# Three changes in a one-core decoder step: an eleven-slot expert ring, an output projection in split products, and a new attention order

## The chip, the cores and the metric

The kernel runs on one core of a Trainium2 chip. The core has a matrix engine (PE in the profile), three engines for elementwise work (DVE, ACT, POOL), and a sequencer (SP) that here only issues DMA transfers. Each engine works through its own list of instructions in program order and meets the others at semaphores, counters that one instruction raises and another waits for. The metric is the device time of one execution in microseconds (us); less is better.

## The reference

One layer of a decoder for 512 prompt tokens and 32 sample tokens (8 sequences of 4, each with 256 cached positions), width 1024, all in float32:

```
h = x @ w_in                                  # 1024 -> 5632: retention q,k,v,g; attention q,k,v; gates a,b
o_r = groupnorm(retention(rq, rk, rv)) * silu(rg)          # 4 heads of 128
o_m = moba(mq, mk, mv)                                     # 8 heads of 64, softmax, past keys in pages
merged = sigmoid(a) * (o_r @ w_br_ret) + sigmoid(b) * (o_m @ w_br_moba)
x1 = layer_norm(ALPHA * x + merged @ w_out)                # the output projection
y  = layer_norm(ALPHA * x1 + moe(x1))                      # 32 experts, 1024 -> 128 -> 1024, 2 per token
```

## The kernel before

The 544 tokens stand as five row tiles (four of 128, one of 32). The stages follow each other.

**Projection of x** (0 to 197 us). Weights come in column tiles of 128. Each float32 operand is split into a high part in a rounded format (fp32r) and a low part, the rest; `split_weights` makes both on DVE. A product is then three matmuls, high by high, high by low and low by high (`split_products`, L677 to L679), each 272 token columns wide.

**Attention** (197 to 296 us). A list `ORDER`, written by hand, gives the steps, and PE, DVE and ACT each walk it and do their share, so its order is the order on all three. `S` is a score product (PE into one of four PSUM banks, DVE takes it out), `R` the normalization of exponentials on DVE, `T` the transposes of the probabilities on PE with a copy by ACT, `O` a product whose result DVE or ACT takes out, `W(m)` the split of weight tile m on DVE, `G(m)` its product on PE, `N` the normalization of the retention rows. The eight MoBA heads go as four pairs: `moba(p)` is the eight scores of pair p, `inv(p)` its `R` steps, `turned(p)` its eight transposes, `pv` its product with the values. `ret`, `rets` and `reto` are scores, state and output of a retention head; `samp`, `skv`, `cross`, `sampv` and `sel` belong to the samples.

**Gates and branches** (to 438 us). 24 tiles: gate a, gate b and branch (r) tiles in turn. PE needs some 6 us for each, DVE splits the next one meanwhile and, after a branch tile, `merge` writes one of the eight slices of `merged`.

**Output projection** (440 to 517 us). For each row tile, both halves of 512 columns and eight slices k, one plain float32 matmul at L928 with `merged` as the stationary operand and `w_out` as the moving one: 80 matmuls. DVE does the layer norm of tile t while PE is at tile t+1; `turn_x1` and `router` stand between on PE.

**Routing and experts** (517 to 678 us). Experts go in 16 pairs; pair n uses experts 2n and 2n+1, each 1.5 MB of weights, of which the gate and up part (1 MB, L634) and the down part (0.5 MB, L629) come by transfers of their own. Eight slots of a ring take experts 0 to 28 in turn; three more places (`cst`, `scratch` and `w_ring`, which are free by then) are loaded once, with experts 29, 30 and 31. Experts 0 to 2 and 31 are loaded while the projection runs, 3 to 7 once it is done, 29 and 30 once routing is known; a slot is refilled when PE is through with it. Token rows are gathered and results scattered by POOL. Then the rows are summed and normalized (to 717 us).

## Time and profile before

| what | value |
|---|---|
| median of three runs | 718.72 us (716.89 to 720.13) |
| time of the profiled execution | 718.71 us |
| span of that execution (first to last instruction) | 716.9 us |
| PE busy | 646.8 us (90%) |
| share of PE in the chain that ended last | 81% |

The span is what the trace shows; the execution's own time is 1.8 us longer, and what the change does to the span is added to that time. A busy PE is one with a matmul in flight; whether it is at its pace is read from the spacing of matmuls.

### The profile page before, as it was taken

To read this page: it belongs to the slowest core of one execution; us is meant where nothing else is said; L and a number is where in the kernel's file an instruction comes from. 1 tells how busy PE (TensorE), PEld (TensorE's weight loads), DVE (VectorE), ACT (ScalarE), POOL (GpSimd) and SP (SyncE) were. 2 spreads that over 40 slices of the span, in tenths; PEclk is the share of its full clock that TensorE was granted. 3 is DMA by queue.
4 is the path that set the end of the run, shared out by engine and by line. 5 is a ranking of instruction groups with operands and counts; after the bars stand their busy time and mean duration, and the time that the engine had idled before them with its cause. 6 is when DMAs were issued, how large, how long until landed. Compare 5 with 4: busy or idle time off the path is not lost.

```text
span 716.9 us, 10905 instructions
## 1 busy us (share of the span) xinstructions
PE 646.8 (90%) x4365; PEld 503.9 (70%) x4365; DVE 291.3 (41%) x585; ACT 133.6 (19%) x286; POOL 70.8 (10%) x74
## 2 busy tenths in 40 slices
PE   4999999999989988799999997999943899988996
PEld 3999999999955666699999995455343455454431
DVE  6344334353275577434444442333365112211235
ACT  0111101120083434300000010000110331312222
POOL 0101400030040000000000000000002133221213
PEclk9999999999999999899999999999955899999996
DMA  9425221227145362233444205900077999998163
GB/s 357 143 88 176 88 88 59 87 74 237 61 114 143 109 180 90 59 89 136 143 144 141 85 1 171 392 30 30 29 300 271 387 407 416 415 417 345 54 267 125
DMA packets 45479, 124.49 MB, mean 174 GB/s; under 512 B 6177, under 2 KB 19617, under 8 KB 41218
## 3 DMA queue, kind: packets, MB, share of 16 engines
q1 hardware_dynamic: 39392, 112.33, 43.4%
q0 software_dynamic: 4752, 8.93, 3.3%
q10 hardware_dynamic: 1298, 2.73, 1.0%
q8 instruction: 25, 0.41, 0.2%
q14 instruction: 12, 0.10, 0.0%
HBM read 114.72 MB, written 17.43 MB: 184 GB/s over the span
## 4 chain that ended last, share of the span: by engine, by line
PE 81%; DVE 8%; DMA 6%; ACT 2%; issue 2%; SPq 1%; POOLq 0%; DVEq 0%; ACTq 0%
PE ps L679 12%; PE ps L677 12%; PE ps L678 12%; PE ps L928 10%; PE ps L970 7%; PE ps L672 6%; PE ps L986 3%; DMA arena<-experts 3%; PE ps L1048 3%; PE ps L891 2%; PE ps L892 2%; PE ps L893 2%; PE ps L743 1%; PE ps L805 1%; PE ps L739 1%
## 5 line engine op out<-in xcount | busy, mean ns | idle before, releaser
L677 PE MATMUL ps<-xa_hi,w_hi 128*128 128x272 f32 x704 | 206.9, 294 | 10.4 <-DVE xa_lo L1370 10.4
L679 PE MATMUL ps<-xa_hi,w_lo 128*128 128x272 f32 x704 | 205.3, 292 | 0.0
L678 PE MATMUL ps<-xa_lo,w_hi 128*128 128x272 f32 x704 | 204.7, 291 | 0.0
L677 PEld LDWEIGHTS ps<-xa_hi,w_hi 128*128 128x128 f32 x704 | 134.7, 191 | 11.8 <-issue 9.8
L678 PEld LDWEIGHTS ps<-xa_lo,w_hi 128*128 128x128 f32 x704 | 134.9, 192 | 0.0
L679 PEld LDWEIGHTS ps<-xa_hi,w_lo 128*128 128x128 f32 x704 | 134.5, 191 | 0.0
L1361 DVE CAST w_hi<-w_ring 128x1024 fp32r<-128x1024 f32 x52 | 38.0, 730 | 121.1 <-PE ps L679 91.0
L928 PE MATMUL ps<-arena 128*128 128x512 f32 (+1 forms) x160 | 70.1, 594 | 2.3 <-issue 2.3
L970 PE MATMUL ps<-arena,work 128*64 128x256 f32 x464 | 60.3, 409 | 8.6 <-DMA arena<-experts 6.4
L1363 DVE TENSOR_TENSOR w_lo<-w_ring,w_hi 128x1024 fp32r<-128x1024 f32 x52 | 65.7, 1263 | 1.8
L970 PEld LDWEIGHTS ps<-arena,work 128*64 128x64 f32 x464 | 37.4, 147 | 27.2 <-issue 9.9
L928 PEld LDWEIGHTS ps<-arena 128*128 128x128 f32 (+1 forms) x160 | 27.3, 174 | 39.9 <-issue 39.8
L1303 POOL DMA_INDIRECT work<-x_rows,idx_i x13 | 13.3, 1027 | 374.4 <-DVE idx_i L1698 339.6
L891 PE MATMUL ps<-o_parts,w_hi 128*128 128x272 f32 x128 | 36.9, 289 | 1.6 <-DVE scratch L1543 1.6
L1381 DVE COPY arena<-ps 128x512 f32 x20 | 13.8, 690 | 59.7 <-PE ps L672 59.7
L893 PE MATMUL ps<-o_parts,w_lo 128*128 128x272 f32 x128 | 36.9, 288 | 0.0
L892 PE MATMUL ps<-o_parts,w_hi 128*128 128x272 f32 x128 | 36.9, 288 | 0.0
L1074 ACT ACTIVATE scratch<-ps 128x544 f32<-128x544 f32 x20 | 12.5, 624 | 126.6 <-PE ps L679 126.6
L1721 DVE COPY work<-ps 128x512 f32<-128x512 f32 x31 | 20.0, 686 | 36.5 <-PE ps L986 36.5
L1153 ACT ACTIVATE scratch<-ps,bm 128x544 f32<-128x544 f32 x16 | 11.5, 716 | 117.7 <-PE ps L679 117.7
L672 PE MATMUL ps<-cst,scratch 128*128 128x128 f32 (+1 forms) x180 | 27.9, 281 | 6.0 <-ACT arena L1121 3.7
L1715 DVE TENSOR_TENSOR work<-work,ps 128x128 f32<-128x128 f32 x16 | 4.6, 288 | 66.6 <-ACT work L1203 66.6
(222 smaller groups left out, 727.0 us busy)
## 6 DMA issues: line engine op xcount, KB each, us to landing
arena<-experts SPq DMA_DIRECT2D x29, 1024.0 KB, 15.9
w_ring<-w_tiles SPq DMA_DIRECT2D x52, 512.0 KB, 3.5
arena<-experts SPq DMA_DIRECT2D x29, 512.0 KB, 19.2
arena<-kT_pool SPq DMA_DIRECT2D x16, 256.0 KB, 3.1
out<-arena SPq DMA_DIRECT2D x4, 1024.0 KB, 5.9
arena<-v_pool SPq DMA_DIRECT2D x16, 256.0 KB, 2.9
arena<-w_out SPq DMA_DIRECT2D x4, 1024.0 KB, 5.6
arena<-token_rows SPq DMA_DIRECT2D x8, 512.0 KB, 6.5
```

The source lines that it names most:

```text
L672: return nc.tensor.transpose(out, in_, ident[0:rows, 0:rows])
L677: mm(out, w_hi[b][:, w], x_hi[:, k_x, cols], start=start, stop=False)
L678: mm(out, w_hi[b][:, w], x_lo[:, k_x, cols], start=False, stop=False)
L679: return mm(out, w_lo[b][:, w], x_hi[:, k_x, cols], start=False, stop=stop)
L891: mm(out, w_hi[m % 2][:, w], o_r[:, hi + k, cols], start=k == 0, stop=False)
L892: mm(out, w_hi[m % 2][:, w], o_r[:, lo + k, cols], start=False, stop=False)
L893: x = mm(out, w_lo[m % 2][:, w], o_r[:, hi + k, cols], start=False, stop=k == 3)
L928: m = mm(ps[0:r, 2 * (t % 2) + half, :], merged[:, k, t * P:t * P + r], wo[:, k, half * 512:(half + 1) * 512], start=k == 0, stop=k == KD - 1)
L970: m = mm(ps[s * CAP:(s + 1) * CAP, 2 + u, 0:2 * P], xgT[:, u, k, s * CAP:(s + 1) * CAP], wgu(slots[s], k), start=k == 0, stop=k == KD - 1)
L986: m = mm(ps[s * CAP:(s + 1) * CAP, 4 + 2 * u + half, :], hidT[:, u, s * CAP:(s + 1) * CAP], wd(slots[s], half), start=True, stop=True)
L1361: v.tensor_copy(w_hi[b][:], w_ring[:, j, :]).then_inc(s_hi, 1)
L1363: v.tensor_tensor(w_lo[b][:], w_ring[:, j, :], w_hi[b][:].bitcast(F32), ALU.subtract).then_inc(done, 1)
```

## The change

It does three things. (1) All eleven places for experts become one ring: expert e goes to place e modulo 11 (`SLOTS`), the place loaded early with expert 31 gets expert 10, the two loaded after routing get 8 and 9, and pair n's places are refilled with experts 2n+11 and 2n+12. PE's loop over pairs is written out. (2) The output projection takes split products: ACT writes the high parts of `w_out` (`wo_high`) and of `merged` (`merged_high`), DVE the low parts (`wo_low`, `merged_low`); five of the eight slices of `w_out` are split during the branch tiles, three after the last gate tile. (3) `ORDER` is new: retention heads come one pair earlier, `turned` is cut in two halves with other steps between, gate tile 0 and then tile 1 stand between the steps of the last pair (before, tile 0 alone stood near its end), with their weights in a buffer of their own (`w_buf`); the last pair's scores use two PSUM banks rather than four.

```diff
+SLOTS = 11
...
+        m_lo, = under(XT, [("merged_lo", [P, KD, T])])
+        wo_early, = under(WO, [("w_out_early", [P, 5, 2, D])])
...
+        wo_late, m_hi = under(0, [("w_out_late", [P, 3, 2, D]), ("merged_hi", [P, 2, KD, P])])
...
-        w_hi, w_lo = [w_hi0, w_hi1], [w_lo0, w_lo1]
+        w_hi, w_lo = [w_hi0, w_hi1, w_hi2], [w_lo0, w_lo1, w_lo2]
...
-        ORDER = ([("S", ("inner",))] + moba(0) + [("S", ("samp", 0))] + O("cross", 0) + inv(0) + skv(0)
-                 + [("R", ("samp", 0))] + turned(0)
-                 + moba(1) + ret(0) + O("pv", 0) + O("rets", 0) + inv(1) + [("T", ("samp", 0))] + O("reto", 0)
-                 + ret(1) + O("sampv", 0) + O("rets", 1) + turned(1) + O("sel", 0) + O("reto", 1)
-                 + moba(2) + ret(2) + O("pv", 1) + [("S", ("samp", 1))] + O("rets", 2) + inv(2) + O("cross", 1)
-                 + O("reto", 2) + ret(3) + [("R", ("samp", 1))] + turned(2) + O("rets", 3) + skv(1) + O("reto", 3)
-                 + moba(3) + O("pv", 2) + [("T", ("samp", 1)), ("N", ("std",)), ("W", (0,))] + inv(3) + O("sampv", 1)
-                 + [("N", ("rows",))] + turned(3) + O("sel", 1) + [("G", (0,))] + O("pv", 3))
...
+        ORDER = ([("S", ("inner",))] + moba(0) + [("S", ("samp", 0))] + O("cross", 0) + ret(0) + inv(0) + O("rets", 0)
+                 + turned(0, 0) + skv(0) + O("reto", 0) + turned(0, 1) + [("R", ("samp", 0))]
+                 + moba(1) + ret(1) + O("pv", 0) + [("T", ("samp", 0))] + O("rets", 1) + O("sampv", 0) + inv(1)
+                 + O("reto", 1) + turned(1, 0) + ret(2) + O("sel", 0) + turned(1, 1) + O("rets", 2) + O("reto", 2)
+                 + moba(2) + ret(3) + O("pv", 1) + [("S", ("samp", 1))] + O("rets", 3) + inv(2) + O("reto", 3)
+                 + turned(2, 0) + O("cross", 1) + skv(1) + turned(2, 1) + [("R", ("samp", 1))] + fill_weights(0)
+                 + moba(3) + O("pv", 2) + [("T", ("samp", 1)), ("N", ("std",))] + fill(0) + inv(3) + O("sampv", 1)
+                 + turned(3, 0) + fill_weights(1) + [("N", ("rows",))] + turned(3, 1) + fill(1) + O("sel", 1) + O("pv", 3))
...
+        LATE = S_IDX[("moba", 3, 0, 0)]
+
         def s_bank(jb):
-            return S_IDX[jb] % 4
+            return S_IDX[jb] % (4 if S_IDX[jb] < LATE else 2)
...
+        def w_buf(m):
+            return 2 if m == 0 or m % 2 == 1 else 1
+
+        def g_bank(m):
+            return 2 if m < 2 or TILES[m][0] == "b" else 0
...
+        def pair_slots(n):
+            return 2 * n % SLOTS, (2 * n + 1) % SLOTS
...
+                if 12 <= m <= 20 and m % 2 == 0:
+                    load_wo((m - 12) // 2)
+            sp.wait_ge(s_tile, M_OF[("b", KD - 1)] + 1)
+            for k in range(5, KD):
+                load_wo(k)
...
+            load_parts(10, experts_d[10])
...
+                load_parts(8 + s, experts_d[8 + s])
+            def next_experts(n):
+                return [e + SLOTS for e in (2 * n, 2 * n + 1) if e + SLOTS < NE]
...
+                for e in next_experts(n):
+                    sp.dma_start(expert(e % SLOTS)[:, 0:GU], experts_d[e][:, 0:GU]).then_inc(s_e[e % SLOTS], 16)
...
+                if k >= LATE:
+                    pe.wait_ge(s_su, k - 1)
+                elif k >= 4:
...
-                if m < 2:
+                if m == 0:
+                    pe.wait_ge(s_su, LATE)
+                elif m == 1:
+                    pe.wait_ge(s_cgs, 1)
+                elif m == 2:
...
+                b = g_bank(m)
+                project_split(w_buf(m), b, 0, xa_hi, xa_lo)
+                project_split(w_buf(m), b + 1, 1, xa_hi, xa_lo).then_inc(s_tile, 1)
...
+            pe.wait_ge(s_wol, 5)
             pe.wait_ge(s_cgs, 16)
+            pe.wait_ge(s_cbu, 9)
...
-                        m = mm(ps[0:r, 2 * (t % 2) + half, :], merged[:, k, t * P:t * P + r],
-                               wo[:, k, half * 512:(half + 1) * 512], start=k == 0, stop=k == KD - 1)
+                        if t == 0 and half == 0:
+                            if k == 0:
+                                pe.wait_ge(s_ml, 1)
+                            elif k == KD - 1:
+                                pe.wait_ge(s_ml, 2)
+                            if k >= 5:
+                                pe.wait_ge(s_wol, k + 1)
+                        elif half == 0 and k == 0:
+                            pe.wait_ge(s_ml, t + 2)
+                        hi, lo = m_hi[:, t % 2, k, 0:r], m_lo[:, k, t * P:t * P + r]
+                        mm(out, hi, wo_part(k, 0)[:, cols], start=k == 0, stop=False)
+                        mm(out, hi, wo_part(k, 1)[:, cols], start=False, stop=False)
+                        m = mm(out, lo, wo_part(k, 0)[:, cols], start=False, stop=k == KD - 1)
...
-            with pe.Fori(1, 3) as i:
-                four_pairs(i)
-            four_pairs(3)
...
+            for n in range(PAIRS):
...
+            def wo_high(k):
+                act.wait_ge(s_wo[k], 16)
+                A(wo_part(k, 0), wo_raw(k), ACT.Identity).then_inc(s_woh, 1)
...
+            def merged_high(t, k0=0, k1=KD):
+                r = P if t < 4 else NS
+                if t >= 2:
+                    act.wait_ge(s_y, t - 1)
+                A(m_hi[:, t % 2, k0:k1, 0:r], merged[:, k0:k1, t * P:t * P + r], ACT.Identity).then_inc(s_mh, 1)
...
+                if 11 <= m <= 19 and m % 2 == 1:
+                    wo_high((m - 11) // 2)
+            for k in range(5, KD):
+                wo_high(k)
+            act.wait_ge(s_mg, KD - 1 + 2)
+            merged_high(0, 0, KD - 1)
+            act.wait_ge(s_mg, KD + 2)
+            merged_high(0, KD - 1, KD)
+            merged_high(1)
...
-                    dve.wait_ge(s_o, max(done("reto", 3), done("cross", 1)))
-                    dve.wait_ge(s_s, used(("samp", 1)))
+                    dve.wait_ge(s_su, used(("ret", 3, 3)))
                 elif m == 1:
+                    dve.wait_ge(s_tile, 1)
+                elif m == 2:
...
+            def wo_low(k):
+                dve.wait_ge(s_woh, k + 1)
+                v.tensor_tensor(wo_part(k, 1), wo_raw(k), wo_part(k, 0).bitcast(F32), ALU.subtract).then_inc(s_wol, 1)
...
+            def merged_low(t, n, k0=0, k1=KD):
+                cols = slice(t * P, t * P + (P if t < 4 else NS))
+                dve.wait_ge(s_mh, n)
+                v.tensor_tensor(m_lo[:, k0:k1, cols], merged[:, k0:k1, cols],
+                                m_hi[:, t % 2, k0:k1, 0:P if t < 4 else NS].bitcast(F32), ALU.subtract).then_inc(s_ml, 1)
...
+                if 13 <= m <= 21 and m % 2 == 1:
+                    wo_low((m - 13) // 2)
+            merge(KD - 2)
+            for k in range(5, KD):
+                wo_low(k)
+            merged_low(0, 1, 0, KD - 1)
+            merge(KD - 1)
+            merged_low(0, 2, KD - 1, KD)
+            merged_low(1, 3)
```

DVE's list ahead of the last pair's first score. Before: the normalization of the second samples, a state copy, four `skv` steps, the copy and statistics of a retention output, then the score (L1403; ISA is the fused score step):

```order
L1436 RECIPROCAL small<-small 128x1
L1455 COPY arena<-ps 128x128
L1422 SCALAR_TENSOR_TENSOR arena<-arena,ps 128x4x128 x4
L1448 COPY arena<-ps 128x4x128
L1450 BN_STATS gstat<-ps 128x6 x4
L1474 BN_AGGR gmv<-gstat 128x2 x4
L1403 ISA scratch,small<-ps,w_ring 128x128
```

In the change, on the same engine and at the same place:

```order
L1514 COPY arena<-ps 128x4x128
L1516 BN_STATS gstat<-ps 128x6 x4
L1540 BN_AGGR gmv<-gstat 128x2 x4
L1526 TENSOR_TENSOR arena<-arena,ps 128x128
L1545 BN_STATS gstat<-arena 128x6
L1546 BN_AGGR gmv<-gstat 128x2
L1488 SCALAR_TENSOR_TENSOR arena<-arena,ps 128x4x128 x4
L1502 RECIPROCAL small<-small 128x1
L1427 CAST w_hi<-w_ring 128x1024
L1429 TENSOR_TENSOR w_lo<-w_ring,w_hi 128x1024
L1469 ISA scratch,small<-ps,w_ring 128x128
```

The retention output has moved ahead of the sample steps, and the split of weight tile 0 (CAST and subtraction) now stands directly in front of the score.

PE's list at the start of the output projection, before: two row tiles in one run, then the transposes of the first.

```order
L928 MATMUL ps<-arena 128x512 x32
L672 MATMUL ps<-cst,arena 128x128 x8
L928 MATMUL ps<-arena 128x512 x8
L915 MATMUL ps<-wr,work 128x36 x8
L928 MATMUL ps<-arena 128x512 x8
```

In the change, the first two slices of the first half row tile:

```order
L977 MATMUL ps<-w_out_early,merged_hi 128x512
L978 MATMUL ps<-w_out_early,merged_hi 128x512
L979 MATMUL ps<-w_out_early,merged_lo 128x512
L977 MATMUL ps<-w_out_early,merged_hi 128x512
L978 MATMUL ps<-w_out_early,merged_hi 128x512
L979 MATMUL ps<-w_out_early,merged_lo 128x512
```

Each former matmul has become three, of the same 512 columns; the transposes and the router products stand where they stood.

## Rows read from the trace of the kernel before

**Rows 1.** Profile page, 40 slices: granted PE clock and DMA share, in tenths.

```profile
PEclk9999999999999999899999999999955899999996
DMA  9425221227145362233444205900077999998163
```

**Rows 2.** Windows: width, busy time (instructions) by engine, granted clock, DMA share, GB/s.

```profile
265.00:300.00 35.00, 27.70 (x176) 20.20 (x177) 24.68 (x69) 15.50 (x38) 0.00 (x0) 0.90 0.34 103
...
340.00:400.00 60.00, 60.00 (x480) 60.00 (x479) 26.87 (x33) 4.32 (x7) 0.00 (x0) 1.00 0.44 148
```

**Rows 3.** Chain that ended last, around the output projection: start, length, work.

```profile
437.94 2.30 issue
440.24 27.70 PE ps L928 x64
...
468.82 6.87 PE ps L928 x16
...
510.50 7.00 PE ps L928 x16
```

**Rows 4.** Groups by line (busy, mean ns), and one group of DMA issues.

```profile
L677 PEld LDWEIGHTS ps<-xa_hi,w_hi 128*128 128x128 f32 x704 | 134.7, 191 | 11.8 <-issue 9.8 <-DVE xa_lo L1370 1.6
...
L1363 DVE TENSOR_TENSOR w_lo<-w_ring,w_hi 128x1024 fp32r<-128x1024 f32 x52 | 65.7, 1263 | 1.8
L1361 DVE CAST w_hi<-w_ring 128x1024 fp32r<-128x1024 f32 x52 | 38.0, 730 | 121.1 <-PE ps L679 91.0 <-PE ps L893 24.4 <-DMA w_ring<-w_tiles 5.7
...
w_ring<-w_tiles SPq DMA_DIRECT2D x52, 512.0 KB, 3.5
```

**Rows 5.** Timeline of DVE at the last two merges: start, length, instruction, idle before.

```profile
431.57 0.73 DVE L1545 TENSOR_TENSOR arena<-arena,scratch 128x544 f32<-128x544 f32 x1
...
438.67 0.71 DVE L1543 TENSOR_TENSOR scratch<-scratch,ps 128x544 f32<-128x544 f32 x1
```

**Rows 6.** Timeline of PE in attention, pieces that begin after a wait.

```profile
207.41 0.98 PE L672 MATMUL ps<-cst,scratch 128*128 128x128 f32 x7 [0.74 <-DVE scratch L1433]
209.66 0.98 PE L672 MATMUL ps<-cst,scratch 128*128 128x128 f32 x7 [0.20 <-ACT arena L1121]
...
265.65 2.02 PE L739 MATMUL ps<-arena 64*128 64x384 f32 x8 [1.32 <-DVE small L1403]
...
271.14 1.92 PE L832 MATMUL ps<-arena 128*32 128x512 f32 x16 [0.68 <-issue]
...
274.82 0.95 PE L672 MATMUL ps<-cst,scratch 128*128 128x128 f32 x7 [0.71 <-DVE scratch L1433]
...
292.39 1.94 PE L672 MATMUL ps<-cst,arena 128*128 128x128 f32 x8 [3.02 <-DVE o_parts L1531]
295.65 0.45 PE L672 MATMUL ps<-cst,arena 128*128 128x128 f32 x1 [1.32 <-DVE o_parts L1531]
```

**Rows 7.** Timeline of DVE: a normalization of half a pair; four sample steps.

```profile
206.08 1.27 DVE L1433 TENSOR_SCALAR scratch<-scratch,small 128x128 f32<-128x128 f32 x4
...
261.06 2.48 DVE L1422 SCALAR_TENSOR_TENSOR arena<-arena,ps 128x512 f32<-128x512 f32 x4 [0.70 <-PE ps L763]
```

**Rows 8.** Timeline of PE: gate and up products of pairs 1, 9, 12, 13.

```profile
565.34 3.67 PE L970 MATMUL ps<-arena,work 128*64 128x256 f32 x32 [1.06 <-ACT work L1198]
...
619.37 3.67 PE L970 MATMUL ps<-arena,work 128*64 128x256 f32 x32
...
647.70 5.04 PE L970 MATMUL ps<-arena,work 128*64 128x256 f32 x32 [2.59 <-DMA arena<-experts]
...
656.08 3.67 PE L970 MATMUL ps<-arena,work 128*64 128x256 f32 x32 [0.19 <-DMA arena<-experts]
```

**Rows 9.** Chain that ended last: the gate and up products of pair 15.

```profile
669.65 3.60 PE ps L970 x32
```

**Rows 10.** Windows of 10 us in the expert stage, columns as in rows 2.

```profile
600.00:610.00 10.00, 10.00 (x80) 5.80 (x77) 2.04 (x5) 1.92 (x5) 3.03 (x3) 1.00 1.03 419
...
660.00:670.00 10.00, 10.00 (x70) 5.18 (x69) 2.43 (x5) 3.06 (x8) 0.98 (x1) 1.00 0.20 80
```

More of the change, by code:

```diff
@@ L290, in hybrid_step @@
         s_idle = sem("idle_written")
-        s_rst = sem("head_state_stored")
+        s_rst = [sem(f"head_state_stored{u}") for u in range(2)]
         s_st = sem("states_loaded")
@@ L333, in hybrid_step @@
         s_mg = sem("merged_ready")
-        s_wo = sem("w_out_loaded")
+        s_wo = [sem(f"w_out_loaded{k}") for k in range(KD)]
+        s_woh = sem("w_out_high_parts")
+        s_wol = sem("w_out_low_parts")
+        s_mh = sem("merged_high_parts")
+        s_ml = sem("merged_low_parts")
         s_x = sem("x_loaded")
@@ L400, in ret @@
             return [("S", ("ret", h, kb)) for kb in range(4)]
-        def turned(p):
-            return [("T", ("moba", p, u, kb)) for u in range(2) for kb in range(4)]
         def inv(p):
@@ L662, in _ @@
             sp.wait_ge(s_x1s, 16 * TT)
-            sp.wait_ge(s_rst, 64)
+            for u in range(2):
+                sp.wait_ge(s_rst[u], 32)
             sp.wait_ge(s_out, 16 * (2 + TT))
@@ L890, in branches @@
                             out = ps[:, 4 + 2 * br_ + half, 0:HALF]
-                            mm(out, w_hi[m % 2][:, w], o_r[:, hi + k, cols], start=k == 0, stop=False)
-                            mm(out, w_hi[m % 2][:, w], o_r[:, lo + k, cols], start=False, stop=False)
-                            x = mm(out, w_lo[m % 2][:, w], o_r[:, hi + k, cols], start=False, stop=k == 3)
+                            mm(out, w_hi[w_buf(m)][:, w], o_r[:, hi + k, cols], start=k == 0, stop=False)
+                            mm(out, w_hi[w_buf(m)][:, w], o_r[:, lo + k, cols], start=False, stop=False)
+                            x = mm(out, w_lo[w_buf(m)][:, w], o_r[:, hi + k, cols], start=False, stop=k == 3)
                 x.then_inc(s_tile, 1)
-            for m in range(1, 3 * KD):
+            for m in range(2, 3 * KD):
                 if TILES[m][0] == "r":
@@ L976, in turn_hidden, with down @@
                 tr(ps[:, 2 + u, 2 * P:3 * P], hid[:, u], P).then_inc(s_ht, 1)
-            def down(n, slots, u, loaded=None):
+            def down(n, slots, u, loaded=True):
                 pe.wait_ge(s_hc, n + 1)
-                for s in slots if loaded is not None else ():
-                    if s < 8:
-                        pe.wait_ge(s_ed[s], loaded)
+                for s in range(2) if loaded else ():
+                    pe.wait_ge(s_ed[slots[s]], 16 * ((2 * n + s) // SLOTS + 1))
                 pe.wait_ge(s_ye, n + 1)
@@ L1126, in copy_probs, with gate_values @@
                     A(pt_n[0:NS, 2, :], ps[0:NS, b, 2 * P:3 * P], ACT.Identity).then_inc(s_tu, 1)
+            def gate_values(m):
+                kind, n = TILES[m]
+                u = 0 if kind == "a" else 1
+                act.wait_ge(s_tile, m + 1)
+                if m == 0:
+                    act.wait_ge(s_o, done("reto", 3))
+                if n >= 2:
+                    act.wait_ge(s_mg, 2 + n - 1)
+                A(gate_s[:, n % 2, u].rearrange("p (h c) -> p h c", h=2), ps[:, g_bank(m):g_bank(m) + 2, 0:HALF], ACT.Sigmoid,
+                  bias=bm[:, 8 * u + n:8 * u + n + 1]).then_inc(s_cgs, 1)
             biases(0)
@@ L1550, in _ @@
                     merge(TILES[m - 2][1])
-            for m in range(3 * KD - 2, 3 * KD):
-                if TILES[m][0] == "r":
-                    merge(TILES[m][1])
+                if 13 <= m <= 21 and m % 2 == 1:
[7 more added lines that the diff above has]
+            merged_low(1, 3)
             def row_stats(n, z, r):
```

114 lines of the change are left out of this document (50 added, 64 removed).

## The prediction, made before the changed kernel had run

> **What bounds the kernel now.** I read the page first: PE is busy 90% of the span and its granted clock is near full except in a short stretch near slice 30, while the DMA line stands at 9 for some five slices in the same part [rows 1]. So PE's own pace sets most of the time, and the transfers may set the expert stage. Then I took each of the three stages that the change touches by itself.
>
> In the gate stage, as far as it is clear of attention, 480 matmuls of 272 columns take 60.00 us at full clock, 125 ns each [rows 2]. At 2.4 GHz that is 300 cycles, 1.10 a column. In the output projection the 80 matmuls of the program show as 160, each of 512 columns: 27.70 us for 64 and 6.87 us for 16, about 430 ns each [rows 3], 1031 cycles or 2.01 a column, twice. Plain float32 thus costs about four cycles a column, one split product about one.
>
> In the experts, pairs 1 to 9 start 54.03 us apart, 6.754 us a pair [rows 8]. Later PE waits for `arena<-experts`, and the DMA engines are full at 419 GB/s [rows 8, 10]. At that pace pair 15 would start at 565.34 + 14 x 6.754 = 659.9; it starts at 669.65 [rows 9]. The transfers cost 9.7 us there.
>
> In attention PE waits in short pieces: 0.74, 1.32, 0.68, 0.71, then 3.02 and 1.32 us at the end [rows 6].
>
> **Output projection.** It removes 160 half-products and puts 240 matmuls in their place. The trace has no fp32r matmul of 512 columns, so I bound its pitch. One cycle a column is 213.3 ns. On top of the cycles for its columns, the 512-column half-product has 430 - 426.7, some 3 ns, and the 272-column split product has 125 - 113.3 = 11.7 ns [rows 2, 3]. The pitch is thus 216 to 225 ns, and I take 216, because the row with the same 512 columns is the nearer one: with so long a stream behind it the next weight load has time to hide. 240 x 0.216 = 51.8 us. The half row tiles of before cost 27.70 + six of 6.87 to 7.00 [rows 3]; with 6.93 as the mean of those six, 69.3 us. Saved: 17.5 us; at 225 ns 15.3.
>
> The Trainium skill (TensorE: Matmul & The Clock Gate, section Back-to-back issue gap) gives the spacing of lone matmuls as columns by 2.4 GHz plus 2.5 ns. By it 240 would take 51.8 us too, but it makes 115.8 ns of the 272-column matmul, where the trace has 125; by the trace's surplus the sum would be 54.0.
>
> What the split costs elsewhere: a slice of `w_out` is as wide as a weight tile, so DVE pays 1.26 us for a low part, and ACT a copy [rows 4]. Five slices go under branch tiles, where PE needs 6 us a tile, ACT is busy 4.32 us in 60 and DVE 26.87 [rows 2]. A tile with a split (1.99) and a merge (three operations like the 0.73 [rows 5], 2.2) then has 5.4 us of DVE work, still under 6; uncovered, it would be 5 x 1.26 us. The last three slices are loaded when gate b's last tile is done, two branch tiles ahead of the projection; a tile of their size lands 3.5 us after its issue [rows 4]. Merge 6 ends at 432.30 [rows 5], then three low parts (3.8) and seven slices of `merged` (1.1) keep DVE to 437.2, before merge 7 can begin at 438.0. So they are hidden, with 0.8 us to spare. The start even comes earlier: before, PE waited for the third operation of merge 7 until 440.24 [rows 3]; now the second, which ends at 439.38 [rows 5], is enough, since the last slice of `merged` is wanted only 21 matmuls (4.5 us) later. Saved 0.8 us. In the row tiles DVE gets one more subtraction of 1.26 us, on some 6 us of work against 10.4 us of PE. Hidden.
>
> **Expert ring.** It moves no byte less. Three places that held experts of the last two pairs now hold 8, 9 and 10, so the refill that brought expert 2n+8 brings 2n+11, wanted one and a half pairs, 10.1 us, later. No wait before was longer in sum than 9.7, so all of it could go. Against that, refills land one behind the other, and with PE on pace the gathers and scatters of pairs 10 to 13 come earlier into the same queue: two scatters of 0.5 MB, 2.5 us at 419 GB/s. The rate falls to 80 GB/s in the window from 660 [rows 10], so the weights have landed by about 661; with 2.5 us more, 663.5, pair 15 starts at latest 3.6 us behind pace. The gain is 6.1 to 9.7. I take 8.0: expert 29 (pair 14, wanted at 653.1) has the place in the queue that expert 26 had, whose pair could start at 656.08 [rows 8]. It lands before its partner by a transfer (1 MB, 2.5 us), and is put off by a gather and a scatter, which makes some 2 us of wait. The written-out loop adds nothing: pair to pair the step is the same inside the loop and where it turns.
>
> **Attention.** PE's work is the same; gate tile 1 only moves ahead of the end. Halves of `turned` with work between save at least the 0.20 us wait between them, four times: 0.8. The waits of 0.68 (samples) and 0.71 (last normalization) now have gate tile 0 in front: 1.4. Lost: in pair 0, DVE does four retention steps before the normalization, worth 0.4 more than the 0.74 of before. The last pair's first score: DVE is late by 1.32 before [rows 6]; the split of tile 0 (1.99 us [rows 4]) now stands in front of it, behind two normalizations (2 x 1.27) and four sample steps (2.48) [rows 7]. The lateness lies between 1.32 and 3.31; I take 2.4, 1.1 more, since PE too has half a chain of transposes, `cross` and `skv` to do in that time. With two banks each score also waits for the one before last to be taken out; between 0 and 2.3 us, I take 1.2. The end is as it was: `pv`, a tile split on DVE, rows, a second split, so the waits of 3.02 and 1.32 stay. Sum: 2.2 saved, 2.7 lost, 0.5 us slower. What is late next is the last pair's probabilities, but PE has gate tile 0 (6 us) for that.
>
> **Sum.** Against the profiled execution's 718.71 us, within 0.01 of the median: 718.7 - 17.5 - 0.8 - 8.0 + 0.5 = **692.9 us**.
>
> **Rivals.**
> 1. *The transfers still end the expert stage.* For it: a full DMA line. Against it: the rank of each refill moves by more than the wait. Gain 6.1: 694.8.
> 2. *Split products keep the 272-column surplus.* Pitch 225 ns: 695.1.
> 3. *The clock falls in the last pair.* PE idles there with little between. After 3.02 us of idle the eight transposes took 1.94 us, and the window's clock is 0.90 [rows 2, 6]; pair 12's products took 5.04 us rather than 3.67 after 2.59 us [rows 8]. Price: 1.4 us by that row, twice that if two bursts are caught: 694.3 to 695.7. Against it: a wait of 1.32 us leaves the scores at their 2.02 us [rows 6], and the wait of 2.4 is broken by a score. The Trainium skill (same page, section HAM oscillation) also says that waits between bursts make the next burst run at half rate; the trace agrees for the two long waits.
> 4. *Slower than before: weight loads in series.* 240 loads instead of 160; if each 191 ns load [rows 4] stood in front of its matmul, the projection would take 51.8 + 45.8 = 97.6 us, 28.3 more, and the kernel 738.7. It decides from a pitch of (69.3 + 8.3) / 240 = 323 ns. Against it: in the gate stage the same loads fit into 125 ns.
> 5. *Attention does fill its holes:* the waits up to the last pair go and the two banks cost nothing: some 4 us less, 689.
>
> **How the numbers follow.** Main case 0.48 (690.5 to 695); rivals 0.12, 0.10, 0.19, 0.02, 0.07; the rest, 0.02, lies below. Rivals 1 to 3 and 5 lie within 687 to 699, where also two of them together fit, so that is the range. About 0.5% (3.6 us) is what a measurement of this kernel tells from no change; only rival 4 gets there, so faster 0.97, same 0.01, slower 0.02.
>
> **What would show it.** Right: a half row tile of 24 matmuls at 5.2 us, the first about 0.8 us earlier behind the last branch tile; pair 15 about 14 x 6.75 us plus at most 3 behind pair 1, with full clock; gate tiles 0 and 1 inside the last pair, with a wait of 2 us or more at its scores. Wrong: 5.4 us or more for a half row tile; waits for `arena<-experts` that remain; a wait for `merged_lo` or `w_out_late` at the projection's start; a granted clock of half around the last pair.

## The result, and the profile after

The changed kernel takes 701.85 us (median of 4, 700.43 to 702.07) against 718.99 for the kernel before (median of 4 on the same chip), ratio 0.9761, 95% interval 0.9734 to 0.9787. It is faster by 17.1 us. The forecast was 26, and the time lies above the range.

The two profiled executions (spans 716.9 and 700.2 us) can be cut at the same four places, so that the 16.7 us between them are shared out:

| stretch | before | after | change | forecast |
|---|---|---|---|---|
| up to the end of the rows' last transpose wait, two gate tiles done | 295.65 + 6.05 (one more gate tile) [rows 6] | 305.46 | +3.8 | +0.5 |
| last branch tile's end to start of pair 1 | 437.94 to 565.34 [rows 3, 8] | 441.63 to 554.65 | -14.4 | -18.3 |
| start of pair 1 to the first product after pair 15 | 565.34 to 679.59 | 554.65 to 664.02 | -4.9 | -8.0 |
| from there to the end | 679.59 to 716.9 | 664.02 to 700.2 | -1.1 | 0 |

Gates and branches, between the first two rows of the table, differ by less than 0.1 us. All three terms came out worse, each by 3 to 4 us. The tail gains 1.1 us because its last eight products took 4.78 us instead of 5.96, at a granted clock of 0.74 instead of 0.59; in the experiments below the same eight take 3.59 to 5.87, so this belongs to the execution.

The slices of the page after, which answer to [rows 1]:

```profile
PE   3999999999999898979999999999942899999886
PEclk9999999999999997989999999999955799999997
DMA  9425322227227435112343302771067999999273
```

PE is still the bound, and the DMA line still stands at 9 in six slices in a row in the expert stage.

**Attention.** PE in the last pair and at the end, in the timeline (start, us, operation, in brackets the wait before it; L773 is now the scores, L831 the products, L704 the transposes), which answers to [rows 6]:

```profile
262.21 1.08 PE L773 MATMUL ps<-arena 64*128 64x128 f32 x4
265.08 1.43 PE L773 MATMUL ps<-arena 64*128 64x256 f32 x4 [1.78 <-DVE small L1469]
266.82 1.99 PE L773 MATMUL ps<-arena 64*128 64x384 f32 x4 [0.31 <-DVE small L1469]
269.13 2.55 PE L773 MATMUL ps<-arena 64*128 64x512 f32 x4 [0.32 <-DVE small L1469]
271.61 3.76 PE L831 MATMUL ps<-arena 128*64 128x512 f32 x16
...
302.20 1.94 PE L704 MATMUL ps<-cst,arena 128*128 128x128 f32 x8 [3.02 <-DVE o_parts L1598]
305.46 0.45 PE L704 MATMUL ps<-cst,arena 128*128 128x128 f32 x1 [1.32 <-DVE o_parts L1598]
```

From the first score to the products of pair 2 it takes 9.40 us; before, 4.21 (263.40 to 267.61). The products take 3.76 us instead of 2.38. The waits of 3.02 and 1.32 at the end are unchanged. DVE at the same place shows the split of tile 0 in front of the first score that it takes out:

```profile
262.86 0.69 DVE L1427 CAST w_hi<-w_ring 128x1024 fp32r<-128x1024 f32 x1
263.59 1.23 DVE L1429 TENSOR_TENSOR w_lo<-w_ring,w_hi 128x1024 fp32r<-128x1024 f32 x1
264.73 0.28 DVE L1469 CUSTOM_DVE_ANT_0 scratch<-ps,w_ring 128x128 f32<-128x128 f32 x1
```

And the windows of this stretch (busy time of PE, PEld, DVE, ACT, POOL, then granted clock, DMA share, GB/s) show PE at its lower level, 1.2 GHz:

```profile
265.00:271.00 6.00, 5.29 (x12) 2.53 (x12) 2.06 (x12) 3.28 (x12) 0.00 (x0) 0.50 0.46 138
271.00:275.00 4.00, 4.00 (x16) 1.30 (x16) 1.31 (x4) 1.52 (x4) 0.00 (x0) 0.57 0.36 76
```

The kernel before has full clock, 2.4 GHz, at this place:

```profile
265.00:275.00 10.00, 7.96 (x47) 3.46 (x48) 7.90 (x31) 7.00 (x21) 0.00 (x0) 1.00 0.69 207
```

**Projection.** Starts of its products in the timeline: the first two, the first of the second and of the third half row tile, and two of the last half row tile, which has 32 columns of weights. They answer to [rows 3].

```profile
443.33 0.47 PE L977 MATMUL ps<-w_out_early,merged_hi 128*128 128x512 f32 x1 [1.70 <-DVE scratch L1610]
443.64 0.39 PE L978 MATMUL ps<-w_out_early,merged_hi 128*128 128x512 f32 x1
...
448.93 0.39 PE L977 MATMUL ps<-w_out_early,merged_hi 128*128 128x512 f32 x1
...
454.42 0.39 PE L977 MATMUL ps<-w_out_early,merged_hi 128*128 128x512 f32 x1
...
500.96 0.39 PE L977 MATMUL ps<-w_out_early,merged_hi 128*32 128x512 f32 x1
...
506.24 0.39 PE L979 MATMUL ps<-w_out_late,merged_lo 128*32 128x512 f32 x1
```

24 products take 454.42 - 448.93 = 5.49 us, 229 ns each. That is 16 ns over the 213.3 of one cycle a column, and over the upper bound of 225. In the last half row tile 23 take 5.28 us, 229.6 ns, though a load of 32 columns takes 109 ns and one of 128 columns 189: the weight load does not set the pitch. Nor does other traffic: with 128 columns of weights the pitch is 229 ns from 444 to 455, at a DMA share of 1.02, and 230 ns from 488 to 492, at 0.06.

**Experts.** The products of pairs 1, 14 and 15 (L1020), and the transposes behind those of pair 15, which answer to [rows 8, 9]:

```profile
554.65 3.67 PE L1020 MATMUL ps<-arena,work 128*64 128x256 f32 x32 [1.07 <-ACT work L1264]
...
643.68 3.67 PE L1020 MATMUL ps<-arena,work 128*64 128x256 f32 x32 [1.17 <-DMA arena<-experts]
...
652.32 0.40 PE L1020 MATMUL ps<-cst,work 128*64 128x256 f32 x1 [1.82 <-DMA scratch<-experts]
...
657.62 1.09 PE L704 MATMUL ps<-cst,work 128*128 128x128 f32 x8
```

PE keeps the pace of 6.754 us to pair 13. Two waits, 1.17 and 1.82, are left; pair 15 starts 652.32 - (554.65 + 14 x 6.754) = 3.1 us late, where before it was 9.7. Its products then take 5.3 us instead of 3.6, since part of them ran at half clock (granted 0.68 from 652.3 to 657.6). The wait and that stretch take 4.8 us of the 9.7 back.

### The profile page after: what moved, and what is told of

Read it like the earlier page. It is cut to its first block, busy times and chain, and to the rows that moved or that the text cites. A ratio compares the mean times of both kernels' runs of the same rounds, so it can differ in the third digit from the quotient of the medians.

```text
span 700.2 us, 11093 instructions
## 1 busy us (share of the span) xinstructions
PE 633.7 (91%) x4445; PEld 516.9 (74%) x4445; DVE 305.4 (44%) x599; ACT 146.2 (21%) x300; POOL 70.1 (10%) x74
## 4 chain that ended last, share of the span: by engine, by line
PE 80%; DVE 7%; DMA 6%; issue 2%; SPq 2%; ACT 2%; DVEq 0%; POOLq 0%; ACTq 0%
PE ps L711 13%; PE ps L709 13%; PE ps L710 13%; PE ps L1020 6%; PE ps L704 5%; DMA scratch<-experts 3%; PE ps L1035 3%; PE ps L977 3%; PE ps L1089 3%; PE ps L979 3%; PE ps L978 3%; PE ps L929 2%; PE ps L931 2%; PE ps L930 2%; PE ps L773 2%
## 5 line engine op out<-in xcount | busy, mean ns | idle before, releaser
L709 PE MATMUL ps<-xa_hi,w_hi 128*128 128x272 f32 x704 | 206.8, 294 | 10.6 <-DVE xa_lo L1436 10.6
L1020 PE MATMUL ps<-arena,work 128*64 128x256 f32 x384 | 49.8, 395 | 3.4 <-ACT work L1264 2.2
L1020 PEld LDWEIGHTS ps<-arena,work 128*64 128x64 f32 x384 | 29.9, 142 | 18.1 <-issue 3.0
L1447 DVE COPY arena<-ps 128x512 f32 x20 | 13.8, 690 | 59.7 <-PE ps L704 59.7
L704 PE MATMUL ps<-cst,scratch 128*128 128x128 f32 (+1 forms) x180 | 27.8, 280 | 5.0 <-ACT arena L1162 3.1
L704 PEld LDWEIGHTS ps<-cst,work 128*128 128x128 f32 x120 | 14.0, 146 | 23.4 <-issue 23.4
L704 PEld LDWEIGHTS ps<-cst,scratch 128*128 128x128 f32 (+1 forms) x180 | 19.4, 136 | 11.7 <-ACT arena L1162 6.6
```

What stands on the lines that cost most here:

```text
L704: return nc.tensor.transpose(out, in_, ident[0:rows, 0:rows])
L709: mm(out, w_hi[b][:, w], x_hi[:, k_x, cols], start=start, stop=False)
L1020: m = mm(ps[s * CAP:(s + 1) * CAP, 2 + u, 0:2 * P], xgT[:, u, k, s * CAP:(s + 1) * CAP], wgu(slots[s], k), start=k == 0, stop=k == KD - 1)
```

## The experiments

Each was run beside the kernel before; the ratio of the changed kernel, 0.9761, is what to hold them against. Ratios have intervals of about 0.002 to 0.006 on either side, so that 2 us are at the edge; the traces tell what the times can't.

**The last pair of attention, in four runs.** Four banks for its scores:

```diff
-        LATE = S_IDX[("moba", 3, 0, 0)]
+        LATE = nS
...
                 if m == 0:
-                    pe.wait_ge(s_su, LATE)
+                    pe.wait_ge(s_su, nS)
```

> The changed kernel, but the last pair's scores keep four banks (gate tile 0 then waits until all scores are taken out, which they are 3 us before it comes). Theory (the split of tile 0 on DVE in front of the scores and the two banks act in series, and the half clock of the stretch 265 to 275 comes only from the waits that they make): the first two steps of scores (0.93 us of before) run at once, the third waits some 1.4 us for DVE as it did before, the clock stays full; the products of pair 2 start near 267.2 instead of 271.6 and take 2.4 us instead of 3.8; in all 5 to 6 us, about 696.3 us against 701.9. Rival 1 (the lateness of DVE alone): the waits only move from the first score to the third, the clock falls all the same; at most 2 us gained, 700 to 702. Rival 2 (the clock falls in this stretch whatever the waits, since transposes and short waits stand before it): waits gone, scores still at half speed; 2 to 3 us gained, about 699.

697.39 us, ratio 0.9674 (0.9650 to 0.9697). PE in the last pair:

```profile
260.88 1.33 PE L773 MATMUL ps<-arena 64*128 64x128 f32 x8
263.79 3.15 PE L773 MATMUL ps<-arena 64*128 64x384 f32 x8 [1.57 <-DVE small L1469]
266.86 2.86 PE L831 MATMUL ps<-arena 128*64 128x512 f32 x16
```

One wait is left, and the clock still falls behind it: 3.15 us for the last two steps of scores (2.02 before). That is rival 1's way, a wait that moves to the third step and half clock behind it. From first score to products it takes 5.98 us instead of 9.40. The gain is nearer to the theory's: 4.3 us in this stretch, part of the rest ahead of it, where this execution was 1.3 us earlier.

The split behind the scores:

```diff
-  ... + [("R", ("samp", 1))] + fill_weights(0) + moba(3) + O("pv", 2)
+  ... + [("R", ("samp", 1))] + moba(3) + fill_weights(0) + O("pv", 2)
```

> The changed kernel, but the split of gate tile 0 stands behind the last pair's scores on DVE instead of in front of them; two banks as changed. Theory (lateness and banks in series): DVE takes the first score out at 262.9 instead of 264.7, each further step of scores waits only the 0.3 us that the two banks cost at any clock, no wait is longer than about 0.7 us, and the clock stays full; the products of pair 2 start near 267.3, in all about 5.5 us, 696.3 us against 701.9; gate tile 0 finds its parts just ready (near 270.1). Rival 1 (two banks alone): the waits stay at 0.3 to 1.8 us, less than 1 us gained. Rival 2 (the clock falls whatever the waits): 2 to 3 us gained, about 699.

698.76 us, ratio 0.9679 (0.9643 to 0.9716). What the scores waited for (us, times), and the window 266 to 270:

```profile
  DVE small L1469: 1.9, 3
  DVE arena L1488: 0.5, 2
```

```profile
266.00:270.00 4.00, 3.92 (x9) 1.29 (x8) 2.27 (x7) 1.72 (x5) 0.00 (x0) 0.50 0.42 120
```

No long wait, but 2.4 us of it in five pieces, and the clock fell all the same: 7.10 us to the products, which took 3.17. The longest piece, 1.23 us at 266.75, came when the clock had fallen already (0.58 from 264 to 265); the pieces ahead of the fall are shorter than 0.5 us. In the trace only 2.9 us are gained, which is rival 2's size. The times of this kernel lie between 694.61 and 700.82, and the profiled one is the longest, with a mean granted clock of 0.950 against 0.952 to 0.961 in the others: these may have kept the clock.

Both edits, the two diffs above in one kernel:

> Four banks for the last pair's scores and the split of gate tile 0 behind them. Theory: the four steps of scores run in about 3 us without a wait over 0.5 us, at full clock; the products of pair 2 start near 265.5 instead of 271.6; with 1.4 us less for them 7 to 7.5 us in all, about 694.5 us against 701.9. Rival (the clock falls whatever the waits): about 698. If either edit alone is all, this one equals it within 1 us.

696.94 us, ratio 0.9667 (0.9638 to 0.9697). PE, and a window:

```profile
262.46 3.07 PE L773 MATMUL ps<-arena 64*128 64x128 f32 x16
265.46 2.38 PE L831 MATMUL ps<-arena 128*64 128x512 f32 x16
```

```profile
262.00:266.00 4.00, 4.00 (x23) 2.35 (x24) 3.86 (x16) 3.21 (x14) 0.00 (x0) 1.00 0.92 262
```

Scores in 3.00 us, products in 2.38, full clock: 7.8 us of this stretch, of which 6.95 reach the rows' last transpose (298.51 instead of 305.46). So the clock does not fall here by itself: it fell when either source of waits was left, and not when both were gone. It fell in all nine profiles of kernels that keep the last pair of the changed kernel: 0.50 to 0.61 from 265 to 271.

The times say less. They show 4.9 us gained where the theory had 7 to 7.5, and the ratio can't be told from that of four banks alone (0.9667 and 0.9674). In the trace the lead of 6.95 us is 6.1 at pair 1, 5.3 behind pair 15 and 4.8 at the end.

The order of before under ring and split projection (the last lines of the list; its start, the four banks and the places of the gate tiles go back likewise):

```diff
...
-                 + moba(3) + O("pv", 2) + [("T", ("samp", 1)), ("N", ("std",))] + fill(0) + inv(3) + O("sampv", 1)
-                 + turned(3, 0) + fill_weights(1) + [("N", ("rows",))] + turned(3, 1) + fill(1) + O("sel", 1) + O("pv", 3))
+                 + moba(3) + O("pv", 2) + [("T", ("samp", 1)), ("N", ("std",)), ("W", (0,))] + inv(3) + O("sampv", 1)
+                 + [("N", ("rows",))] + turned(3, 0) + turned(3, 1) + O("sel", 1) + [("G", (0,))] + O("pv", 3))
```

> The changed kernel with the order of attention of the kernel before (its four banks, one gate tile before the last pair's products, the other behind the rows); ring and split projection stay. Theory (the new order costs 3.7 us as the traces stand: the last transposes of the rows end at 305.5 with two gate tiles done, before at 295.7 with one, a gate tile being 6.05): 698 us, ratio to before 0.971. Rival (the new order costs nothing, the missing microseconds are in the two other parts): 701.9.

697.86 us, ratio 0.9682 (0.9650 to 0.9715), as the theory had it. The last pair is as before (score to products 4.20 us, waits of 1.32, 0.68, 0.71), and behind the wait of 1.32 the scores keep full clock:

```profile
263.65 0.93 PE L773 MATMUL ps<-arena 64*128 64x128 f32 x8
265.89 2.02 PE L773 MATMUL ps<-arena 64*128 64x384 f32 x8 [1.32 <-DVE small L1469]
```

Its last transpose is at 295.88 with one gate tile done, so 301.9 with two: the changed order loses 3.5 us to it as it stands, and gains 3.4 with the two edits above.

**Gate tile 1 between the rows' transposes** (on DVE the split of tile 3 moves behind the rows):

```diff
-  ... + turned(3, 1) + fill(1) + O("sel", 1) + O("pv", 3)
+  ... + turned(3, 1) + O("sel", 1) + O("pv", 3)
...
             for t in range(TT):
+                if t == 2:
+                    gate(1)
                 pe.wait_ge(s_gn, t + 1)
```

> The changed kernel, but gate tile 1 stands between the second and the third transposes of the rows, where PE waits 3.02 and then 1.32 us for DVE, instead of ahead of the last products of attention, where PE waits for nothing; the split of tile 3, which must follow gate tile 1, moves behind the rows. Theory (a gate tile is worth the waits in front of which it stands, and the half clock behind them): the last transpose ends 4.5 us earlier with as many tiles done, the 1.3 us of half clock behind go too; 4.5 to 6 us gained, about 696.5. Rival (DVE's own chain of rows, copies and splits ends the stage): the waits move to the first transposes of the rows, less than 1.5 us gained.

697.22 us, ratio 0.9702 (0.9652 to 0.9753):

```profile
299.36 1.23 PE L704 MATMUL ps<-cst,arena 128*128 128x128 f32 x8 [0.51 <-DVE o_parts L1601]
301.50 0.30 PE L704 MATMUL ps<-cst,arena 128*128 128x128 f32 x1 [0.91 <-DVE o_parts L1601]
```

Waits of 0.51 and 0.91 instead of 3.02 and 1.32, last transpose 4.0 us earlier, full clock behind it (1.00 from 302 to 306), and 4.6 us by the times: the theory stands. In the changed kernel this tile stood where PE waited for nothing, and earned nothing.

**The ring undone** (the first loads go back to experts 29 to 31 likewise):

```diff
+        def place(e):
+            return (e % 8, e // 8 + 1) if e < NE - 3 else (e - NE + SLOTS, 1)
...
         def pair_slots(n):
-            return 2 * n % SLOTS, (2 * n + 1) % SLOTS
+            return place(2 * n)[0], place(2 * n + 1)[0]
```

> The changed kernel with the places of the experts as before: a ring of eight, and 29, 30 and 31 in three places of their own, loaded at the places in the queue where they were loaded before; pairs written out one by one as in the changed kernel. Theory (the ring is worth what the two traces show from the start of pair 1 to the end of pair 15's products, 113.4 against 108.5 us): 4.9 us slower than the changed kernel, ratio to before 0.983, about 706.8. Rival (the ring is worth the 8.0 us of the prediction, and something else in the stage costs 3): 710.

706.78 us, ratio 0.9840 (0.9783 to 0.9897), 4.9 us slower than the changed kernel by the medians, though the two intervals just touch. The trace is sharper. Pairs 1 and 15 start at:

```profile
552.97 3.67 PE L1023 MATMUL ps<-arena,work 128*64 128x256 f32 x32 [1.06 <-ACT work L1267]
...
657.27 0.43 PE L1023 MATMUL ps<-scratch,work 128*64 128x256 f32 x1
```

Pair 15 is 9.7 us late again, and from the start of pair 1 to the end of pair 15's products it takes 107.9 us, as in the kernel before (107.85) and 4.9 more than in the changed one (102.97). In the view of waits the experts' weights now cost PE 7.7 us, where the changed kernel has 3.0:

```profile
PE ps L1023 <- DMA arena<-experts: 7.7, 5, 2.9
```

**Refills by deadline:**

```diff
+            for e in range(SLOTS, NE):
+                refill_gate_up(e)
+                if e % 2 == 1:
+                    for d in (e - 3, e - 2):
+                        if d >= SLOTS:
+                            refill_down(d)
...
```

> The changed kernel with the refills in the order in which PE wants them: gate and up of both experts of a pair, then the down products of both experts of the pair before it. So gate and up of expert 29 goes ahead of the down parts of 25 and 26, that of 31 ahead of the down part of 28. Theory (the queue is full, so the bytes that must land before pair 15 set its start, and the order moves only one down part, 0.5 MB or 1.3 us, behind it): the wait of 1.17 us at pair 14 goes, pair 15 still waits some 1.7 us and starts 1.3 us earlier than 652.3, its products again at half clock; 1 to 1.5 us gained, about 700.6. Rival (the order alone makes the waits): both waits and the slow stretch of 1.7 us go, 4.5 us or more gained, 697 or less.

700.48 us, ratio 0.9748 (0.9695 to 0.9801), no difference. Pairs 14 and 15:

```profile
644.56 3.67 PE L1024 MATMUL ps<-arena,work 128*64 128x256 f32 x32 [2.05 <-DMA arena<-experts]
...
652.92 0.40 PE L1024 MATMUL ps<-cst,work 128*64 128x256 f32 x1 [1.54 <-DMA scratch<-experts]
```

The rival falls: both waits are still there, 0.9 us longer at pair 14 and 0.3 shorter at pair 15 (whose products kept full clock in this execution). The theory, by which the first wait goes and 1.3 us are gained, is not borne out either.

**Fewer bytes ahead of the last transfer.**

```diff
-  sp.dma_start(expert(e % SLOTS)[:, GU:EW], experts_d[e][:, GU:EW]) ...
+  to = GU + 64 if e in (27, 28) else EW
+  sp.dma_start(expert(e % SLOTS)[:, GU:to], experts_d[e][:, GU:to]) ...
```

> The changed kernel, but of the down parts of experts 27 and 28, which stand in the queue right ahead of gate and up of expert 31, only the first 64 of 1024 columns are loaded (the rest of those weights is left out of the result): 0.94 MB less, 2.3 us at 410 GB/s, nothing else changed. Theory (pair 15 waits because of the bytes ahead of its last transfer, and its products run at half clock because PE waited): its weights land near 650, the wait at pair 15 shrinks from 1.8 us to nothing, pair 14's wait of 1.2 us stays, pair 15 starts near 650.4 instead of 652.3 and its products take 3.7 us instead of 5.4: 3 to 3.6 us gained, about 698.5. Rival 1 (the wait is that of one slow transfer or of the queue's end, whatever stands ahead): no gain. Rival 2 (the clock falls there by itself): 1.9 us gained, products still at 5.4 us.

698.74 us, ratio 0.9707 (0.9670 to 0.9744). Pair 15 without a wait, and the window over its end:

```profile
650.54 0.43 PE L1021 MATMUL ps<-cst,work 128*64 128x256 f32 x1
```

```profile
640.00:664.00 24.00, 21.03 (x123) 10.42 (x124) 5.14 (x9) 8.24 (x21) 3.90 (x4) 1.00 0.44 176
```

Pair 14 still waits (1.72 us), and pair 15 starts at 650.54, 1.8 us late, and takes 3.6 us at full clock. So it is the bytes in the queue ahead of it that make pair 15 late. That its wait makes the half clock is not shown by this run: seven profiles of other runs have a wait there and full clock behind it. They also speak against rival 2: the clock does not always fall there.

**The pitch of 229 ns, in four runs.** All use the 240 products of the projection with one thing changed. The upper halves of the words as bf16:

```diff
+  hi, lo, wh, wl = (x.bitcast(mybir.dt.bfloat16)[:, 1::2] for x in (hi, lo, wh, wl))
...
```

> The changed kernel, but the 240 products of the output projection read the upper halves of the same words as bf16 (every second 16-bit element of the same tiles), so the sums lose their low bits; loads, columns and instructions are the same in number. The pitch of 512 columns is 229 ns in the changed kernel, with 128 columns of weights as with 32 (whose load takes 109 ns instead of 188), so the load isn't it. Theory (the surplus of 15.6 ns over 213.3 belongs to the reading of fp32r): pitch 214 to 217 ns, 3 us gained, about 699. Rival (it belongs to any matmul with weights of its own, in any type): pitch 229 ns, no gain.

702.26 us, ratio 0.9757 (0.9704 to 0.9810). The first and last product of one half row tile:

```profile
474.18 0.39 PE L979 MATMUL ps<-w_out_early,merged_hi 128*128 128x512 bf16 x1
...
479.37 0.39 PE L981 MATMUL ps<-w_out_late,merged_lo 128*128 128x512 bf16 x1
```

23 steps in 5.19 us, 225.7 ns, with a load of 97 to 101 ns instead of 189. The type is worth some 3 ns of the 16; the rest stays, and the theory falls. (These operands lie two elements apart; bf16 that lies densely was not run.) The two halves in turn, each with its own bank:

```diff
+  for n, (x, part) in enumerate(((hi, 0), (hi, 1), (lo, 0))):
+      for half in range(2):
+          m = mm(ps[0:r, 2 * (t % 2) + half, :], x, wo_part(k, part)[:, half * 512:(half + 1) * 512], ...
```

> The changed kernel, but the two halves of a row tile of the projection run interleaved: each product for columns 0 to 511 is followed by the same one for columns 512 to 1023 in the other bank, so no two neighbours add into one bank and every second matmul has the weights of the one before. Theory (the surplus of 12 to 16 ns at 512 columns, which neither the load nor the type explains, comes from neighbours adding into one bank): pitch near 216 ns, 3 us gained, about 699. Rival (it belongs to every matmul record with weights of its own): 229 ns, 701.9.

702.49 us, ratio 0.9746 (0.9702 to 0.9789). 48 products from the first to the second row tile:

```profile
444.14 1.16 PE L977 MATMUL ps<-w_out_early,merged_hi 128*128 128x512 f32 x4 [1.70 <-DVE scratch L1609]
...
455.40 1.09 PE L977 MATMUL ps<-w_out_early,merged_hi 128*128 128x512 f32 x4
```

11.26 us, 235 ns: worse, not better, and the trace has a load of weights for each product, also where they are those of the one before. The theory falls. Quarters of 256 columns:

```diff
-  for half in range(2):
+  for half, quarter in ((0, 0), (0, 1), (1, 0), (1, 1)):
...
```

> The changed kernel, but each product of the projection in two of 256 columns, 480 matmuls instead of 240. It measures how the surplus goes with the columns: 28 cycles at 272, 37 at 512. If it is the same for every matmul (37 cycles): 122 ns each, 58.6 us for all instead of 55.0, 3.6 us slower. If it goes with the columns (7%): 114.4 ns each, no change. By the line through the two (about 18 cycles and 4% of the columns), which I hold likeliest: 118 ns, 56.7 us, 1.7 us slower, about 703.6.

702.35 us, ratio 0.9763 (0.9727 to 0.9799). 24 products:

```profile
444.98 0.28 PE L978 MATMUL ps<-w_out_early,merged_hi 128*128 128x256 f32 x1
...
447.83 0.28 PE L978 MATMUL ps<-w_out_early,merged_hi 128*128 128x256 f32 x1
```

2.85 us, 119 ns or 285 cycles each, as the line through the two other sizes had it. Each product a sum of its own:

```diff
-  mm(out, hi, wo_part(k, 0)[:, cols], start=k == 0, stop=False)
+  mm(out, hi, wo_part(k, 0)[:, cols], start=True, stop=True)
...
```

> The changed kernel, but each of the 240 products of the projection starts a sum of its own, so that nothing is added to what the bank holds (the result keeps only the last product; loads, columns and instructions are the same). Theory (the surplus of 16 ns at 512 columns is the reading back of the bank for the addition): pitch near 216 ns, a half row tile of 24 in 5.2 us. Rival (it lies in the streaming itself, some 17 cycles and 4% of the columns, as the three sizes 256, 272 and 512 say): pitch 229 ns, 5.5 us.

Measured once, 704.63 us beside 716.39. From one half row tile to the next, 24 products:

```profile
450.55 0.39 PE L977 MATMUL ps<-w_out_early,merged_hi 128*128 128x512 f32 x1
...
456.04 0.39 PE L977 MATMUL ps<-w_out_early,merged_hi 128*128 128x512 f32 x1
```

5.49 us, 229 ns. The addition isn't it either.

**What the runs point to, together:** four banks, the split behind the scores, gate tile 1 between the rows' transposes, and on DVE two low parts of the rows ahead of the split of tile 2. To the diffs above it adds:

```diff
-            split_tile(2)
             for t in range(TT):
...
                 if t == 2:
+                    split_tile(2)
...
+            split_tile(3)
```

> The changed kernel with what the runs so far point to: four banks for the last pair's scores, the split of tile 0 behind them, gate tile 1 between the second and the third transposes of the rows, and on DVE the first two low parts of the rows ahead of the split of tile 2. Theory (the holes are separate, so their prices add: 6.9 us by the two first edits, 4.2 by the gate tile, and 1 for the split that no longer stands before the rows): ratio to before 0.960, about 690. Rival (one hole filled opens the next, since DVE's rows come later than PE wants them): 693 to 695.

688.05 us (median of 6), ratio 0.9562 (0.9533 to 0.9590), 2.0% below the changed kernel.

```profile
262.97 3.07 PE L773 MATMUL ps<-arena 64*128 64x128 f32 x16
265.97 2.37 PE L831 MATMUL ps<-arena 128*64 128x512 f32 x16
...
292.62 1.04 PE L704 MATMUL ps<-cst,arena 128*128 128x128 f32 x8
294.89 0.30 PE L704 MATMUL ps<-cst,arena 128*128 128x128 f32 x1 [1.23 <-DVE o_parts L1601]
```

The last transpose is 10.6 us earlier than in the changed kernel, the granted clock from 286 to 310 is 1.00, where the changed kernel has 0.74 from 305 to 312, and pair 1 starts 12.0 us earlier. By the times 13.8 us are gained where the theory had 12.1: the prices add, and the rival falls. The third of them, 1 us, was not measured by itself.

## Why the prediction was right in sign and wrong in size

**Output projection, the pitch.** This step failed. "I take 216, because the row with the same 512 columns is the nearer one": that row was of plain float32, and it did not carry over. The pitch is 229 ns, outside both bounds; 240 x 13 ns are 3.1 us. The bounds themselves were too narrow: they took the surplus as either 3 or 11.7 ns, whatever the length, while it grows with it (12 ns at 256 and 272 columns, 16 at 512). The Trainium skill (TensorE: Matmul & The Clock Gate, section Back-to-back issue gap) gives the spacing of lone matmuls as columns by 2.4 GHz plus 2.5 ns; the estimate by it, 215.8 ns, is off by the same 13 ns, and the measurement decides. Rival 2 had the right idea with too low a price.

**Projection, the rest.** Right. The first product waits 1.70 us behind the last branch tile where it was 2.30 before, 0.6 gained of the 0.8 forecast. The low part of the first slices of `merged` ends on DVE at 440.40, 1.2 us before the last branch tile does. Row tile follows row tile in 13.71 us (routers at 485.54 and 499.25) with no wait.

**Expert ring.** The direction was right, the size not: 4.9 us instead of 8.0, below the lower bound of 6.1. Two things failed. The first is the clock, which the term put at nothing: pair 15 came 3.1 us late in this execution, inside the "at latest 3.6", but its products took 1.7 us more at half clock. The 9.7 us of before had such a price in them, 3.1 us in pairs 10 and 12 [rows 8]; pair 10:

```profile
629.46 5.36 PE L970 MATMUL ps<-arena,work 128*64 128x256 f32 x32 [3.26 <-DMA arena<-experts]
```

The second is the bound itself, and that it held here was luck. In the twelve profiles of kernels with the ring of eleven and all its bytes, pair 15 is 3.0 to 6.75 us late, more than 3.6 in nine. From the start of pair 1 (which is earlier in some of them, at 542.7 to 556.2) to the end of pair 15's products they take 101.5 to 104.9 us against 107.85 before, so the ring is worth 2.9 to 6.3. Five of them have the half clock at pair 15, those with waits of 1.82 to 1.98 us in front of it. The seven with 1.36 to 1.80 kept full clock, and so did pair 14 behind waits of up to 2.42, so the length of the wait does not decide alone. The five are not the longest as a whole (102.9 to 103.9). Rival 1, that transfers still end the stage, is what came, at 4.9 us instead of the 6.1 that it was priced at.

**Attention.** This step failed by a term that the sum put at nothing, the clock. Its places were right: the gate tile hides the waits of 0.68 and 0.71, the end keeps its 3.02 and 1.32, the last pair starts 1.2 us earlier (262.21 instead of 263.40), and the waits come at the scores. The waits themselves were priced too high. They grew from 1.32 us to 2.41 (1.78, 0.31 and 0.32), by 1.1 where "1.1 more" for the lateness and "I take 1.2" for the two banks make 2.3; with four banks the one wait left is 1.57, so the lateness alone makes some 0.25. Yet the stretch up to the products took 5.2 us more, and the products 1.4. The last two steps of scores took 1.99 + 2.55 where both took 2.02 before, so 2.5 us of it are clock in the scores, and with the products 3.9; the 1.6 us beyond waits and clock were not taken apart. The clock was left to rival 3, at 1.4 to 2.8 us, and the argument against that rival, that a score breaks the wait, did not hold. The Trainium skill (TensorE: Matmul & The Clock Gate, section HAM oscillation — how this bites in real kernels) has bursts behind waits run at half rate. The traces agree for these scores, with 7.10 us where short waits were left and 3.00 where none were, but not for every wait: behind the 1.32 us in the order of before the clock stayed at 1.00.

One reading was off besides. PE has work between the halves of `turned` in three pairs, not four: in the last pair only a split on DVE stands there, and the wait of 0.20 stayed (at 286.98). So 0.6 of the 0.8 us could go.

**The chances.** Rivals 1, 2 and 3 were priced as if mostly one would come. All three came, and each beyond its own price: with 225 ns, 6.1 and 2.8 us the sum would have been 692.9 + 2.2 + 1.9 + 2.8 = 699.8. The tail's 1.1 us, which no term had, made the miss smaller by luck. Of the four signs of being wrong that the prediction named, three came: 5.49 us for a half row tile, waits for `arena<-experts`, and half clock around the last pair.

## What to carry to other kernels

A short wait on PE can cost twice, once for itself and once for the products behind it at half clock. It did so behind 1.6 and 1.8 us at the scores and behind 1.8 to 2.0 at pair 15, and not behind 1.3 at the scores or 2.4 at pair 14, so the second price belongs into the range of a forecast and not at nothing. Removing one of two causes of waits in a stretch may leave the clock where it was; removing both gave it back here. A lead won early need not arrive: of 6.95 us won in attention by two edits 4.8 were left at the end. Work that is to fill holes earns only what stands right behind it: the same gate tile was worth nothing ahead of products that waited for nothing, and 4 us between the transposes. A matmul's pitch at a new length is best bounded by rows of its own type and structure, and with a wider bound where there are none.

## What the runs showed of the hardware

At full clock, products with weights of their own took 119 ns at 256 columns, 125 at 272 and 229 at 512: about 17 cycles and 1.04 cycles a column, by a line through the three. At 512 columns the load's length (109 or 189 ns), the DMA share (0.1 or 1.0) and the addition in the bank change nothing; bf16, every second element, takes 225.7 ns; two banks in turn take 235. A half-product of plain float32, 1031 cycles for 512 columns [rows 3], has only 7 over two cycles a column. What the 4% are was not found.
